# Two transformer blocks in float32: mixers rebuilt by head pairs, with two-pass float32r scores and normalised probabilities

## The chip, the cores and the metric

The kernel runs on one core of a Trainium2 chip. The metric is the device time of one execution in microseconds; three timed runs and one profiled execution of the kernel before are given. TensorE (PE) multiplies, VectorE (DVE), ScalarE (ACT) and GpSimd (POOL) do element work, SyncE (SP) issues most DMAs. Every engine works through its own instruction list in order, and the lists are tied together by semaphores that the kernel sets and waits for by hand.

## What is computed

Two different transformer blocks, one after the other, on 512 tokens of width 1024, all float32:

```python
# block 1: 12 heads of 64, three dilated branches (one table of log counts), RoPE, a pooling mixer of width 256
h = rms_norm(x, ln_pre_mix);  proj = h @ w_in                     # 1024 -> 256 + 3*768
mix = concat([multi_scale_pool(u), dilated_attention(rope(q), rope(k), v)]) @ w_out
x = x + rms_norm(mix);  x = x + rms_norm((silu(h2 @ w_gate) * (h2 @ w_up)) @ w_down)
# block 2: three kinds of attention; every q and k head is RMS-normed and scaled by a gain
a = softmax(q1 k1' + alibi) - lam * softmax(q2 k2' + alibi);  o_a = rms_norm(a @ v)     # 4 heads, 8 maps
o_b = softmax(q k' + F_q - F_k, causal) @ v                                             # 6 "fox" heads
o_c = softmax(q k' + rel_bias, chunks) @ v                                              # 6 "chk" heads
h = h + concat([o_a, o_b, o_c]) @ w_out_2;  h = h + conv_gated_mlp(rms_norm(h))
h = h + (p @ w_ple_proj) * sigmoid(rms_norm(h) @ w_ple_gate)
```

All attention is causal in steps, so of a map of 512 by 512 scores only 1, 2, 3 and 4 tiles of 128 keys are computed for the four blocks of 128 queries. There are 12 maps in block 1 and 8 + 6 + 6 = 20 in block 2.

## The kernel before

Everything stays in SBUF between the stages; only weights stream in, 1 MB at a time, into one of two slots (`w_raw`). Each large product is made in three float32r passes: a float32 number is split into a high part (`w_hi`, `h_hi`) and a rest (`w_lo`, `h_lo`), and hi*hi + hi*lo + lo*hi is summed in PSUM (`products`, lines 1337 to 1339; `row_tile`, lines 1482 to 1486). ACT makes the high part of weights (`split_hi`, L707), DVE the rest (`split_lo`, L932), in four quarters of 128x512 a chunk.

The order of the work is one list of steps for each mixer (`block1_plan`, `block2_plan`), and all engines walk through that same list, each doing its share of a step. The steps: `proj` (24 matmuls, 128 tokens by 256 columns; 9 chunks in block 1 and 15 in block 2, four tiles of tokens each), `rows` (DVE reads the bank: RoPE, norm or copy), `qkT` (PE turns q and k, DVE copies them out of bank 7, L1420 and L1062 to L1078), and for one unit, which is a map `m` and a block of queries `t`: `S` (scores in plain float32 from 64 feature rows, L1450; DVE adds the table and takes the maximum, L1171; ACT exponentiates in place, L764), `T` (PE turns the unnormalised probabilities, L1458; ACT copies them out, L771), `PV` (plain float32, the probabilities stationary and 64 columns of values moving, L1470; DVE scales by the reciprocal of the sum, L1184), and `mixT` (the finished heads turned, L1430). A unit's `T` comes two units behind its `S`, its `PV` three behind. The scores use two banks of PSUM by turns, the turned probabilities two more, the projections two, `PV` bank 6 and every other turn bank 7. The maps of a group of four to eight begin when three to five chunks are projected, with the projections of the next group between their units; the last group has the pool mixer or nothing between its units. `out` (0 to 3) are the first row products of `w_out`, put into the end of the list.

POOL has only small norms, the window means of the pool mixer (L639 to L653) and some DMAs.

Of the kernel before, what the change touches and what calls it, by code (L numbers as in the profile page):

```python
# [7 lines left out]
P = 128  # L8
S = 512
T = S // P  # L10
# [29 lines left out]
LEAD = 3  # L40
SECOND_MAP = (3, 1, 2, 0)

NORMED = ("diff_qk", "fox_qk", "chk_qk")
TURNED = ("q", "k") + NORMED

def parts(steps, heads):

    out = []
    for step in steps:  # L50
        if step[0] in heads or not out:
            out.append([])
        out[-1].append(step)
    return out

def interleave(attention, filler):

    units, fillers = parts(attention, ("S",)), parts(filler, ("proj", "poolproj", "poolmix"))  # L60
    out, done = [], 0
    for n, unit in enumerate(units):
        want = len(fillers) * (n + 1) // len(units)
        out += unit + sum(fillers[done:want], [])
        done = want
    return out + sum(fillers[done:], [])

def attention_steps(units, after):

    out = []
    for n in range(max([len(units) + 3] + [m + 4 for m in after])):
        if 0 <= n - 2 < len(units):
            out.append(("T", units[n - 2]))
        if n < len(units):
            out.append(("S", units[n]))
        if 0 <= n - 3 < len(units):
            out.append(("PV", units[n - 3]))
        out += after.get(n - 3, [])  # L80
    return out

def mixer_steps(groups, after, fillers, last_fillers):

    units = [u for maps in groups for m in maps[::2] for t in range(T) for u in ((m, t), (m + 1, SECOND_MAP[t]))]  # L90
    main = attention_steps(units, after)
    starts = [main.index(("S", (maps[0], 0))) for maps in groups]
    out = []
    for lo, hi, filler in zip(starts, starts[1:], fillers):
        out += interleave(main[lo:hi - LEAD], filler) + main[hi - LEAD:hi]
    lo, end = starts[-1], main.index(("S", units[-1])) + 2
    cuts = [lo + (end - lo) * n // len(last_fillers) for n in range(len(last_fillers) + 1)]
    for lo, hi, filler in zip(cuts, cuts[1:], last_fillers):
        out += interleave(main[lo:hi], filler)
# [3 lines left out]

def projection_steps(chunks, ends, extra=None):

# [1532 lines left out]
```

## Time and profile before

| | us |
|---|---|
| median of three runs | 1466.72 |
| lowest and highest | 1466.27, 1471.14 |
| span of the profiled execution | 1469.6 |
| TensorE busy in it | 1428.1 (97%) |
| VectorE / ScalarE / GpSimd busy | 714.2 / 525.4 / 125.8 |

The mixer of block 1 fills about 15 to 244 us of the span, that of block 2 about 656 to 996 us; between and behind them lie the output products and the two feed-forward parts. "Busy" PE time includes a modelled end of each matmul, so a row's mean is longer than the distance from one matmul to the next; the distance is read from the starts in the timeline.

### The profile page before, as it was taken

To read this page: it belongs to the slowest core of one execution; us is meant where nothing else is said; L and a number is where in the kernel's file an instruction comes from.
4 is the path that set the end of the run, shared out by engine and by line. 5 is a ranking of instruction groups with operands and counts; after the bars stand their busy time and mean duration, and the time that the engine had idled before them with its cause. 6 is when DMAs were issued, how large, how long until landed. Compare 5 with 4: busy or idle time off the path is not lost.

```text
span 1469.6 us, 21588 instructions
## 1 busy us (share of the span) xinstructions
PE 1428.1 (97%) x8040; PEld 1212.9 (83%) x8040; DVE 714.2 (49%) x1565; ACT 525.4 (36%) x1066; POOL 125.8 (9%) x205
## 2 busy tenths in 40 slices
PE   6999999899999999999999999999899999999999
PEld 6888877788888888879888899878888888888888
DVE  5655543632322333355546665445555555633454
ACT  4233343432222222343244344453533433423352
POOL 2000050300000000033302221000000000000000
PEclk9999999899999999999999999999999999999999
DMA  6111021232332322223210112103223223232312
GB/s 213 58 59 58 31 85 58 73 101 86 113 99 84 103 101 99 86 86 101 87 59 30 58 31 101 58 1 132 72 86 114 86 97 103 86 115 86 105 44 82
DMA packets 91225, 122.15 MB, mean 83 GB/s; under 512 B 3883, under 2 KB 81146, under 8 KB 90896
## 3 DMA queue, kind: packets, MB, share of 16 engines
q1 hardware_dynamic: 89616, 114.72, 23.5%
q0 software_dynamic: 1536, 6.45, 1.2%
q8 instruction: 47, 0.77, 0.2%
q14 instruction: 26, 0.21, 0.0%
HBM read 119.06 MB, written 2.10 MB: 82 GB/s over the span
## 4 chain that ended last, share of the span: by engine, by line
PE 52%; DVE 1%; POOL 1%; issue 1%; ACT 0%; DVEq 0%; ACTq 0%
PE ps L1337 10%; PE ps L1339 10%; PE ps L1338 10%; PE ps L1482 4%; PE ps L1484 4%; PE ps L1486 4%; PE ps L1450 4%; PE ps L1470 3%; PE ps L1458 2%; PE ps L1348 1%; POOL qk_rs L584 1%; DVE h_tok L967 0%; PE ps L1416 0%; PE ps L1420 0%; POOL qk_ss L583 0%
## 5 line engine op out<-in xcount | busy, mean ns | idle before, releaser
L932 DVE TENSOR_TENSOR w_lo<-w_raw,w_hi 128x512 fp32r<-128x512 f32 x416 | 269.8, 687 | 329.5 <-ACT w_hi L707 329.2
L707 ACT ACTIVATE w_hi<-w_raw 128x512 fp32r<-128x512 f32 x416 | 238.1, 621 | 307.9 <-PE ps L1486 192.8
L1337 PE MATMUL ps<-h_hi,w_hi 128*128 128x512 f32 (+1 forms) x752 | 288.2, 383 | 0.0
L1338 PE MATMUL ps<-h_lo,w_hi 128*128 128x512 f32 (+1 forms) x752 | 287.3, 382 | 0.0
L1339 PE MATMUL ps<-h_hi,w_lo 128*128 128x512 f32 (+1 forms) x752 | 287.2, 382 | 0.0
L1337 PE MATMUL ps<-w_hi,h_hi 128*128 128x256 f32 x896 | 262.5, 293 | 3.3 <-DVE work L1044 1.8
L1339 PE MATMUL ps<-w_hi,h_lo 128*128 128x256 f32 x896 | 255.0, 285 | 0.0
L1338 PE MATMUL ps<-w_lo,h_hi 128*128 128x256 f32 x896 | 254.9, 284 | 0.0
L1482 PE MATMUL ps<-w_hi,st_hi 128*128 128x512 f32 x464 | 181.5, 391 | 0.8 <-DVE st_lo L1197 0.7
L1484 PE MATMUL ps<-w_lo,st_hi 128*128 128x512 f32 x464 | 181.2, 391 | 0.0
L1486 PE MATMUL ps<-w_hi,st_lo 128*128 128x512 f32 x464 | 181.1, 390 | 0.0
L1337 PEld LDWEIGHTS ps<-w_hi,h_hi 128*128 128x128 f32 x896 | 173.3, 193 | 5.6 <-issue 3.4
L1338 PEld LDWEIGHTS ps<-w_lo,h_hi 128*128 128x128 f32 x896 | 173.4, 194 | 0.0
L1339 PEld LDWEIGHTS ps<-w_hi,h_lo 128*128 128x128 f32 x896 | 173.0, 193 | 0.0
L1337 PEld LDWEIGHTS ps<-h_hi,w_hi 128*128 128x128 f32 x752 | 143.2, 190 | 27.4 <-issue 0.9
L1339 PEld LDWEIGHTS ps<-h_hi,w_lo 128*128 128x128 f32 x752 | 143.0, 190 | 27.0
L1338 PEld LDWEIGHTS ps<-h_lo,w_hi 128*128 128x128 f32 x752 | 143.1, 190 | 26.7
L764 ACT ACTIVATE prob<-prob,neg_max 128x128 f32<-128x128 f32 (+3 forms) x128 | 71.9, 562 | 197.4 <-DVE neg_max L1171 197.2
L1482 PEld LDWEIGHTS ps<-w_hi,st_hi 128*128 128x128 f32 x464 | 87.5, 189 | 19.5 <-issue 1.1
L1486 PEld LDWEIGHTS ps<-w_hi,st_lo 128*128 128x128 f32 x464 | 87.5, 189 | 18.2
L1484 PEld LDWEIGHTS ps<-w_lo,st_hi 128*128 128x128 f32 x464 | 87.4, 188 | 18.1
L771 ACT ACTIVATE probT<-ps 128x128 f32<-128x128 f32 (+3 forms) x128 | 54.2, 423 | 21.3 <-PE ps L1458 20.6
(180 smaller groups left out, 1425.7 us busy)
## 6 DMA issues: line engine op xcount, KB each, us to landing
w_raw<-in_w_up_dram SPq DMA_DIRECT2D x33, 1024.0 KB, 5.1
w_raw<-in_w_in_dram SPq DMA_DIRECT2D x25, 1024.0 KB, 5.3
w_raw<-in_w_down_dram SPq DMA_DIRECT2D x22, 1024.0 KB, 4.8
w_raw<-in_w_gate_dram SPq DMA_DIRECT2D x11, 1024.0 KB, 5.2
w_raw<-in_w_out_dram SPq DMA_DIRECT2D x8, 1024.0 KB, 4.8
w_raw<-in_w_ple_gate_dram SPq DMA_DIRECT2D x4, 1024.0 KB, 5.6
x<-in_x_dram SPq DMA_DIRECT2D x4, 512.0 KB, 8.0
out_dram<-x SPq DMA_DIRECT2D x16, 128.0 KB, 1.7
```

Source lines behind the costliest of these rows:

```text
L707: act.activation(w_hi[:, slot, q], w_raw[:, slot, q], ACT.Copy).then_inc(hi_done, 1)
L764: act.activation(prob, prob, ACT.Exp, bias=neg_max[:, u % 8:u % 8 + 1], scale=-1.0, accum_out=den[:, u % 8:u % 8 + 1]).then_inc(exp_done, 1)
L771: act.activation((probT1, probT2)[mx.b][:, u % 2, 0:kn], ps[:, 4 + u % 2, 0:kn], ACT.Copy)\
L932: dve.tensor_tensor(w_lo[:, slot, q], w_raw[:, slot, q], w_hi[:, slot, q].bitcast(F32), ALU.subtract).then_inc(lo_done, 1)
L1337: pe.matmul(out_, s_hi, m_hi, start=(n == 0), stop=False)
L1338: pe.matmul(out_, s_hi, m_lo, start=False, stop=False)
L1339: mm = pe.matmul(out_, s_lo, m_hi, start=False, stop=(n == len(pairs) - 1))
L1450: pe.matmul(ps[:, 2 + u % 2, 0:P * (t + 1)], q[:, P * t:P * t + P], k[:, 0:P * (t + 1)], start=True, stop=True).then_inc(scores_done, 1)
L1470: mm = pe.matmul(ps[:, 6, 0:HD], probT[:, u % 2, P * j:P * j + P], v[:, j, :], start=(j == 0), stop=(j == t))
L1482: pe.matmul(bank, rows_hi[:, k, tok], hi[:, k, col], start=first and k == 0, stop=False, skip_group_check=True)
L1484: pe.matmul(bank, rows_hi[:, k, tok], lo[:, k, col], start=False, stop=False, skip_group_check=True)
L1486: mm = pe.matmul(bank, rows_lo[:, k, tok], hi[:, k, col], start=False, stop=last and k == RB - 1, skip_group_check=True)
```

## The change

Only the two mixers, the weights that feed them and the places of their buffers change.

- **Projection by head pairs.** A chunk is q, k and v of one pair of heads (384 columns; 512 for two differential heads, 262 for the differential values with the forget gates), loaded in two halves of four k-blocks. Each half is a `proj` of 12 matmuls for each tile of tokens; four banks (0 to 3) hold the four tiles.
- **Weight rests on POOL.** `weights_lo` (POOL) takes the place of DVE's `split_lo` in the mixers, in two pieces a load.
- **Scores in two float32r passes.** `turn` turns q or k of a pair for all tokens through bank 7; ACT copies the high part of each head into its rows of a ring tile, DVE writes the rest beside it, into the other 64 rows. For keys both parts are copied once more, so that q (hi over lo) times two stacked key tiles gives all products in two passes of 128 rows. Fox maps have a third pass for the decay.
- **Probabilities normalised first.** `N`: DVE takes the reciprocal, POOL multiplies the probabilities by it; in the differential maps `N2` (DVE) combines the two maps, so that one turn and one `PV` remain for two.
- **Split values stationary.** `T` turns into the single bank 6, ACT copies the high part (`pt_hi`), DVE the rest (`E`, `pt_lo`). `PV` is one step a map: 8 float32r matmuls of 512 down to 128 columns into bank 7; ACT and DVE add its two halves straight into `mixT`, so the `mixT` turns are left out except for the differential heads, which keep a float32 `PVd`.
- **Order.** Units start when their own pair is turned, at 1.1 (block 1) or 1.4 (block 2) units a projection slot.

```diff
+    for k, chunk in enumerate(chunks):
+        ...
+            for half in range(2):
+                for t in range(T):
+                    slots.add(n, ("proj", k, half, t))
+                    n += 1
...
+        ready[k] = n + (3 if normed else 2)
...
+        place = max(place + 1 / rate, ready[chunk_of(u[0])])
+        at.append(int(place))
...
+                    elif kind == "N":
+                        u, kn = mx.unit[s[1:]], P * (s[2] + 1)
+                        pool.wait_ge(rden_done, of["N"] + 1)
+                        p = prob[:, u % NPROB, 0:kn]
+                        pool.tensor_tensor(p, p, rden[:, u % 8:u % 8 + 1].to_broadcast([P, kn]), ALU.mult)\
+                            .then_inc(normed, 1)
...
+            def weights_lo(mx, n, piece):
+                c = mx.c0 + n
+                ...
+                pool.wait_ge(hi_done, 4 * c + 2 * (piece + 1))
+                q = half_piece(mx, n, piece)
+                pool.tensor_tensor(w_lo[:, c % 2, q], w_raw[:, c % 2, q], w_hi[:, c % 2, q].bitcast(F32), ALU.subtract)\
+                    .then_inc(lo_done, 2)
...
+                for i, tile in enumerate(tiles):
+                    rows, others = head_rows(i)
+                    dve.wait_ge(turn_hi_done, 2 * of["turn"] + i + 1)
+                    ins = dve.scalar_tensor_tensor(out=ring[rows if key else others, tile + key, :], in0=ps[rows, 7, :],
+                                                   scalar=turn_scale(mx, g, rows), in1=ring[rows, tile, :].bitcast(F32),
+                                                   op0=ALU.mult, op1=ALU.subtract)
+                ins.then_inc(bank7_read, 1)
...
+                    elif kind == "E":
+                        t = s[2]
+                        dve.wait_ge(pt_hi_done, mx.cnt.of["T", s[1], t]["six"] + 1)
+                        rows = slice(P * t, P * t + P)
+                        dve.tensor_tensor(pt_lo[:, 0:t + 1, rows], ps[:, 6, 0:P * (t + 1)].rearrange("p (j n) -> p j n", n=P),
+                                          pt_hi[:, 0:t + 1, rows].bitcast(F32), ALU.subtract).then_inc(pt_lo_done, 1)
...
+                        if fox:
+                            pe.matmul(bank, nid[:, m - 8:m - 7].to_broadcast([P, P]), ft[:, keys], start=True, stop=False)
+                        pe.matmul(bank, q, ring[:, tile + 1, keys], start=not fox, stop=False)
+                        pe.matmul(bank, q, ring[:, tile + 2, keys], start=False, stop=True).then_inc(scores_done, 1)
+                    elif kind in ("T", "T2"):
+                        ...
+                        if of["six"]:
+                            pe.wait_ge(pt_hi_done, of["six"])
+                        if of["E"]:
+                            pe.wait_ge(pt_lo_done, of["E"])
...
+                        pe.wait_ge(bank7_read, of["seven"])
+                        for j in range(T):
+                            v, later = vs[:, (pair + 1) % 3, j, hh, :], slice(P * j, S)
+                            pe.matmul(ps[:, 7, later], v, pt_hi[:, j, later], start=j == 0, stop=False,
+                                      skip_group_check=True)
+                            mm = pe.matmul(ps[:, 7, later], v, pt_lo[:, j, later], start=False, stop=j == T - 1,
+                                           skip_group_check=True)
```

Three places of the order. First PE in the mixer of block 1, where the maps of the first pair end: before, the end of the first maps' units among projections (`v`, `probT`, `qk` are values, turned probabilities and turned q and k).

```order
L1420 MATMUL ps<-ident,work_70 128x128 x2
L1450 MATMUL ps<-qk_66 128x128
L1470 MATMUL ps<-v_67,probT_69 128x64 x3
L1458 MATMUL ps<-ident,prob_68 128x128 x4
L1450 MATMUL ps<-qk_66 128x128
L1470 MATMUL ps<-v_67,probT_69 128x64 x3
L1458 MATMUL ps<-ident,prob_68 128x128
```

After the change the turn of the second pair's keys (L1604) stands directly ahead of the first map's PV (L1668, L1670; `vs` is the split values), and both use bank 7.

```order
L1604 MATMUL ps<-ident,work_75 128x128 x4
L1668 MATMUL ps<-pt_hi,vs 128x512
L1670 MATMUL ps<-pt_lo,vs 128x512
L1668 MATMUL ps<-pt_hi,vs 128x384
L1670 MATMUL ps<-pt_lo,vs 128x384
L1668 MATMUL ps<-pt_hi,vs 128x256
L1670 MATMUL ps<-pt_lo,vs 128x256
L1668 MATMUL ps<-pt_hi,vs 128x128
L1670 MATMUL ps<-pt_lo,vs 128x128
L1658 MATMUL ps<-ident,prob 128x128 x4
```

Eight PV matmuls took the place of the many small ones, and between two uses of bank 7 there is nothing on PE.

Second, PE at the end of the mixer of block 1, behind the row product `out 1`, after the change.

```order
L1658 MATMUL ps<-ident,prob 128x128 x3
L1644 MATMUL ps<-ring_83 128x512
L1645 MATMUL ps<-ring_83 128x512
L1658 MATMUL ps<-ident,prob 128x128 x2
L1644 MATMUL ps<-ring_83 128x384
L1645 MATMUL ps<-ring_83 128x384
L1658 MATMUL ps<-ident,prob 128x128
L1644 MATMUL ps<-ring_83 128x256
L1645 MATMUL ps<-ring_83 128x256
L1668 MATMUL ps<-pt_hi,vs 128x512
```

Between one `T` (L1658, bank 6) and the next stand only the two score passes of a later unit (L1644, L1645).

Third, POOL as the first attention units of block 1 begin, after the change (before, POOL had nothing here between its DMAs and the window means).

```order
L795 TENSOR_TENSOR w_lo<-w_raw,w_hi 128x768 x6
L745 TENSOR_TENSOR prob<-prob,rden 128x512
L795 TENSOR_TENSOR w_lo<-w_raw,w_hi 128x768
L745 TENSOR_TENSOR prob<-prob,rden 128x384
L795 TENSOR_TENSOR w_lo<-w_raw,w_hi 128x768
L745 TENSOR_TENSOR prob<-prob,rden 128x256
L745 TENSOR_TENSOR prob<-prob,rden 128x128
```

The rests of the weights and the probabilities' normalising now share one queue.

## Rows read from the trace of the kernel before

**Rows 1.** The page: its first lines, busy us (share) and instructions.

```profile
span 1469.6 us, 21588 instructions
PE 1428.1 (97%) x8040; PEld 1212.9 (83%) x8040; DVE 714.2 (49%) x1565; ACT 525.4 (36%) x1066; POOL 125.8 (9%) x205
```

**Rows 2.** Windows of the middle of both mixers: length, busy us (instructions) by engine, clock, DMA.

```profile
60.00:221.00 161.00, 160.11 (x1069) 129.98 (x1069) 86.80 (x297) 59.28 (x162) 18.68 (x24) 1.00 0.16 53
733.00:962.00 229.00, 228.14 (x1655) 195.62 (x1653) 131.57 (x471) 100.08 (x270) 37.13 (x58) 1.00 0.16 54
```

**Rows 3.** Timeline of PE, projection: start, us, then the start of the next.

```profile
22.94 0.28 PE L1338 MATMUL ps<-w_lo,h_hi 128*128 128x256 f32 x1
23.06 0.28 PE L1339 MATMUL ps<-w_hi,h_lo 128*128 128x256 f32 x1
```

**Rows 4.** Timeline of PE, 512 columns in the row products.

```profile
540.56 0.39 PE L1486 MATMUL ps<-w_hi,st_lo 128*128 128x512 f32 x1
540.79 0.39 PE L1482 MATMUL ps<-w_hi,st_hi 128*128 128x512 f32 x1
```

**Rows 5.** Timeline of PE, units of the last maps with no filler.

```profile
953.97 0.28 PE L1458 MATMUL ps<-ident,prob 128*128 128x128 f32 x1
954.18 1.12 PE L1450 MATMUL ps<-qa 64*128 64x512 f32 x2
955.23 1.10 PE L1470 MATMUL ps<-va,probT 128*128 128x64 f32 x8
956.17 0.28 PE L1458 MATMUL ps<-ident,prob 128*128 128x128 f32 x1
956.38 0.70 PE L1450 MATMUL ps<-qa 64*128 64x256 f32 x2
957.01 0.43 PE L1470 MATMUL ps<-va,probT 128*128 128x64 f32 x2
957.28 0.60 PE L1458 MATMUL ps<-ident,prob 128*128 128x128 f32 x4
957.82 0.70 PE L1450 MATMUL ps<-qa 64*128 64x256 f32 x2
```

**Rows 6.** Groups by line and form: count, busy us, mean ns, idle before.

```profile
L1243 DVE SCALAR_TENSOR_TENSOR act_gate<-ps,conv_cols,act_gate 128x510 f32<-128x510 f32 x22 | 16.5, 749 | 2.6
L1171 DVE CUSTOM_DVE_ANT_0 prob<-ps,table 128x384 f32<-128x384 f32 x14 | 7.7, 553 | 3.6 <-PE ps L1450 3.6
L771 ACT ACTIVATE probT<-ps 128x512 f32<-128x512 f32 x32 | 18.7, 585 | 8.4 <-PE ps L1458 8.4
L764 ACT ACTIVATE prob<-prob,neg_max 128x384 f32<-128x384 f32 x32 | 19.7, 615 | 54.0 <-DVE neg_max L1171 53.9
L764 ACT ACTIVATION_READ_ACCUMULATOR prob<-prob,neg_max 128x1 f32 x128 | 23.9, 187 | 0.0
L640 POOL TENSOR_TENSOR pool_a<-pool_u 128x511 f32<-128x511 f32 x2 | 2.1, 1037 | 0.2
L653 POOL TENSOR_TENSOR pool_d<-pool_d,pool_u 128x512 f32<-128x512 f32 x2 | 2.5, 1272 | 0.2
```

**Rows 7.** End of block 1's mixer: windows as in rows 2, then PE's timeline.

```profile
221.00:243.00 22.00, 19.47 (x91) 15.74 (x90) 8.49 (x26) 6.66 (x16) 0.00 (x0) 0.84 0.00 1
...
226.00:228.00 2.00, 2.00 (x9) 1.68 (x9) 0.30 (x2) 0.98 (x3) 0.00 (x0) 0.50 0.00 0
...
224.54 0.99 PE L1470 MATMUL ps<-v,probT 128*128 128x64 f32 x4 [1.70 <-DVE otok L1184]
```

**Rows 8.** One instruction's line: ns min/median/max; POOL's addition and DVE's scaling in the norms.

```profile
L609 POOL TENSOR_TENSOR x<-x,y_scaled x8: 725/1321/1445, 273.0 to 658.6; 128x256 f32<-128x256 f32 x8
L967 DVE SCALAR_TENSOR_TENSOR h_tok<-x,x_rs,gain_pre x20: 1279/1286/1752, 6.8 to 1410.0; 128x1024 f32<-128x1024 f32 x20
```

**Rows 9.** Timeline of all engines: a score product and DVE's reading of it.

```profile
977.77 1.12 PE L1450 MATMUL ps<-qa 64*128 64x512 f32 x2
...
978.93 0.69 DVE L1171 CUSTOM_DVE_ANT_0 prob<-ps,table 128x512 f32<-128x512 f32 x1 [0.96 <-PE ps L1450]
```

More of the change, by code:

```diff
@@ L69, in attention_steps @@
[L69 to L99, printed above, removed]
-    t1, pv1 = main.index(("T", units[-1])), main.index(("PV", units[-1]))
-    out += main[end:t1] + [("out", 0)] + main[t1:pv1] + [("out", 1)] + main[pv1:pv1 + 1] + [("out", 2)]
-    return out + main[pv1 + 1:] + [("out", 3)]
@@ new lines, with columns @@
+KH = KB // 2
+PAIRS = 6
+NPROB = 4
+FALLING = (3, 2, 1, 0)
+POOL_PARTS = 4
+CAUSAL_TABLE = 4
+def columns(chunk):
+    kind = chunk[0]
+    if kind == "qkv":
+        return [(256 + 768 * j + P * chunk[1], P) for j in range(3)]
+    if kind == "pool":
+        return [(0, 256)]
+    if kind == "d":
+        return [(256 * j + P * chunk[1], P) for j in range(4)]
+    if kind == "dv":
+        return [(DIFF_V, 256), (FOX_GATE, 6)]
+    base = FOX if kind == "fox" else CHK
+    return [(base + 384 * j + P * chunk[1], P) for j in range(3)]
@@ L191, in __init__ @@
             kind = s[0]
-            if kind in ("proj", "poolproj", "poolmix"):
+            if kind in ("proj", "out") or kind == "poolproj" and s[3] == POOL_PARTS - 1:
                 self.n["product"] += 1
+            if kind == "rows" or kind == "poolproj" and s[3] == POOL_PARTS - 1:
                 self.n["bank"] += 1
-            elif kind in ("qkT", "mixT", "decay"):
-                self.n["turn"] += 1
-            elif kind == "S":
-                self.n["unit"] += 1
-            elif kind == "out":
-                self.n["product"] += 1
+            if kind in ("turn", "PV", "PVd", "mixT", "decay", "poolmix"):
+                self.n["seven"] += 1
+            if kind in ("turn", "S", "sum", "E", "T2", "N", "N2", "PV", "PVd", "combine"):
+                self.n[kind] += 1
+            if kind in ("T", "T2"):
+                self.n["six"] += 1
+            if kind == "turn" and s[2] % 2:
+                self.n["keys"] += 1
 def two_blocks_kernel(nc, A, out):
@@ new lines, in two_blocks_kernel, with raw_count, more_dmas, chunk_of_map @@
+        m.buffer_free = {key: consumer.get(u - NPROB) for key, u in m.unit.items()}
+        mixers.append(m)
+    dmas = [1] * C_END
+    for m in mixers:
+        for n, (k, kb0, kbs) in enumerate(m.loads):
+            dmas[m.c0 + n] = len(columns(m.chunks[k]))
+    def raw_count(c):
+        return 16 * sum(dmas[c % 2:c + 1:2])
+    def more_dmas(b, slot):
+        first = (C_UP1, C_UP2)[b]
+        c = first + (slot - first) % 2
+        return raw_count(c) - (8 * c + 16 - 8 * (c % 2))
+    def chunk_of_map(b, m):
+        if b == 0:
+            return chunks1.index(("qkv", m // 2))
+        return chunks2.index(("d", m // 4) if m < 8 else ("fox", (m - 8) // 2) if m < 14 else ("chk", (m - 14) // 2))
```

1153 lines of the change are left out of this document (651 added, 502 removed).

## Prediction

> **What bounds the kernel now.** I read the page first: PE is busy for 97% of a span of 1469.6 us, DVE for 49%, ACT for 36%, POOL for 9% [rows 1]. Then the windows of the two mixers, since only they change: between 60 and 221 us PE is busy 160.1 of 161 us, between 733 and 962 us 228.1 of 229; DVE is at 54 and 57% there [rows 2]. So in the mixers nothing waits for anything but PE, and a change is worth what it takes off PE's list, less what it makes PE wait. Then the timeline, for the distance from one matmul to the next, which is what a matmul costs.
>
> **Prices on PE.** A 256-column float32r matmul comes every 0.12 us [rows 3], a 512-column one every 0.23 (0.227 over several) [rows 4]; the slope is 0.42 ns a column, so 384 columns cost 0.173 and 262 cost 0.122. From starts in the unit stretch [rows 5]: S 1.05 us for 512 keys and 0.63 for 256, so 0.84 for 384 and 0.42 for 128, in sum 2.94 for a map. PV: 0.94 for eight small matmuls and 0.27 for two, so 0.49 and 0.72 between, 2.42 a map. T: 0.21 for one turn, 0.54 for four, 1.5 a map. A map costs 6.9 us of PE, and 32 of them 220.
>
> **What leaves PE.**
> - Projection: before 24 chunks of 96 matmuls, 2304 x 0.120 = 276.5. After 1152 of 384 columns, 192 of 512, 96 of 262: 199.3 + 43.6 + 11.7 = 254.6. Gain 21.9, 18 of it in block 2, which projected overlapping columns; wider matmuls alone give little, because the time is nearly all columns.
> - Scores: a map is two passes of 512, 384, 256 and 128 columns. No row shows a float32r matmul of 128 columns. Lower bound the slope (0.067), upper half the float32 pair of S at 128 keys (0.21); I take 0.12, the 256-column row, its nearest. With 0.1 for the change of mode (an estimate: the fixed part of the two matmuls of S is 0.21 in rows 5) the map is 1.68. 32 maps: 94.1 to 53.8, plus a third pass in six fox maps, 3.8. Gain 36.5.
> - PV: 24 maps x (8 matmuls, 1.28, + 0.1) = 33.1, and the differential heads, now one float32 PV for two maps, 4 x 2.42 = 9.7; before 77.4. Gain 34.6.
> - Turns of probabilities: 4 maps fewer, 6.0. Turns of q and k: 52 pairs of 0.32 and 12 fours of 0.54, 23.1, become 32 fours, 17.3: 5.8. mixT: 12 of 14 leave, 6.5.
> - Against it: 24 more beginnings of a group of projections at the same 0.1, 2.4, and 1 for the decay's small products.
>
> Sum: 21.9 + 36.5 + 34.6 + 6.0 + 5.8 + 6.5 - 3.4 = **108 us** less work on PE, about 36 in block 1 and 72 in block 2. The 118 float32r matmuls of 128 columns make it 98 to 114.
>
> **Do the other engines carry it?** For a head pair of block 1 PE needs 26.8 us (16.6 projection, 1.1 turns, 9.1 for two maps). DVE: RoPE and the value rests 6.8, ring rests 4 x 0.75 and key copies 2 x 0.55, scores 2 x 2.3, reciprocals 1.2, `E` 2 x 1.95, PV 2 x 0.69, together 22; ACT 18.6 (exponentials 2 x 3.0, copies of probabilities 2 x 1.7, of PV 1.2, of the ring 3.6, of values 1.1, weights 3.3), by [rows 6]. POOL: a 512-wide operation takes 1.04 to 1.27, so a 768-wide weight rest about 1.6, four of them and two maps of normalisation at 3.1 give 12.6. Though DVE is freed of the weight rests, its share rises to about 80%. In block 2 a fox pair comes to 27 us of DVE and 15 to 21 of POOL in 30 to 32 of PE. So no engine takes PE's place as the bound by its sum. The gain can be lost only in **waits**.
>
> **What PE now waits for.** Before, two banks held scores, two the turned probabilities, and PV had its own. After, all turned probabilities go through bank 6, and turns of q and k, PV, PVd, mixT, poolmix and decay through bank 7, each alone in it. The order shows where two uses follow closely.
> - *Bank 7 behind a turn.* ACT's two copies of 512 (0.585 and, overlapped, 0.49), DVE's second rest 0.75, and handovers of 0.1 [rows 6, 9] give 2.2 if ACT is free; but in ACT's list the exponential of the newest unit (0.6 + 0.19) stands ahead. I take 2.6; bounds 1.9 and 3.4. Behind PV (ACT 0.585, DVE 0.69) 1.7. Against the PE work standing between, block 1 has nine short places: four with nothing between (a turn of keys directly ahead of a PV, 2.6 each), one of 2.05, four of 0.5 to 0.7: 14.7. Block 2 has fifteen: six of 2.6, three of 1.13 in the first differential chunk, the rest 0.2 to 1.9: 23.6.
> - *Bank 6.* The next T waits for ACT's copy and DVE's `E`, and `E` stands behind the newest unit's scores in DVE's list: S 0.45, handover 0.1, table and maximum 0.63, `E` 0.49, handover: 1.75 behind a T. Where no projection lies between, PE has only S, 0.35 to 0.55. 14 places in block 1 (14.0), 19 in block 2 (21.3), half of this in the two tails, where the eight last units have only three row products as filler.
>
> Taken together, since a wait for one bank also lets the other empty, 28 and 45: **73 us**. With round trips 0.7 as long it is 42, with 1.3 as long 110. Queued behind PE's wait is everything: projections, and with them the weights that ACT and POOL prepare.
>
> The drain of the last map (T, `E`, PV, both readers, `out 3`) is longer than before by some 3 us for both mixers; nothing to nine is possible. Start of the kernel: the first half chunk has less to split, but its second half waits for POOL; 0, between -1 and +2.
>
> **The clock.** Before, one wait of 1.70 us that ended at 224.5 was followed by a window at clock 0.50, that is 1.2 GHz in place of 2.4, and the 22 us from 221 to 243 had a mean of 0.84 [rows 7]: 0.16 x 22 = 3.5 us of lost work, some 7 us at the lower level. The change puts about 14 waits of two us or more into streams of projections. But where PE waits anyway, a slow clock costs less. I take five such falls, **17 us**; bounds 0 and 48.
>
> **The sum.** 1469.6 - 108 + 73 + 3 + 17 = 1454.6 of span. The median of the runs lay 2.9 under the profiled span; so **1452 us**.
>
> **POOL beside DVE.** In the norms POOL's 128x256 addition took 725 ns at best and 1445 at worst, DVE's scaling with two SBUF inputs 1279 and 1752, where they ran beside each other [rows 8]. In the mixers before, POOL was almost idle; now it works half the time beside DVE's RoPE sums, key copies and `N2` (two SBUF inputs, or a copy within SBUF).
> The Trainium skill, SBUF — State Buffer, section "Who interferes with whom", says that these two share a pair of ports as an exclusive lock and that the later one is blocked for the whole instruction; the maxima in rows 8 agree with it in kind. That rule speaks against moving weight rests to POOL, and is what the second rival below would rest on.
>
> **Rivals.**
> 1. *Not faster, by the clock.* Each of 14 long waits starts a stretch at 1.2 GHz: 48 in place of 17, span 1485.6, **1483 us**. It decides once more than nine falls occur (108 - 73 - 3 = 32 us is what they have to eat, 3.5 each). For it: rows 7. Against: many falls would overlap. 0.22.
> 2. *Slower, by POOL and DVE holding each other up.* Some 96 DVE operations of the kinds named above, blocked for 0.3 to 0.5 us each on the average, 29 to 48 us; that DVE can carry, but it lies in the round trips of both banks and makes them 1.3 as long: 110 in place of 73, span 1491.6, **1489 us**. It decides when round trips grow by a quarter. 0.15.
> 3. *The queues hide it.* ACT and DVE catch up while PE projects, turns cost 1.9, waits 42, no fall: 1469.6 - 108 + 42 + 3, **1404 us**. For it: ACT is at 70% of PE's work in a pair and DVE at 80, so both have time to catch up. 0.22.
> 4. *The forecast*, 1435 to 1465: 0.41.
>
> **Range and chances.** 1400 to 1503 takes in the third case down to its own value, both slow ones and 10 us for the narrow matmuls, and leaves out the sum of all good ends (1395 and less) and of all bad ones. What a measurement of this kernel can tell from no change is 0.3%, 4.4 us. Faster: the third case, and nearly all of the forecast's, 0.59. Same: 0.08. Slower: 0.33, from rivals 1 and 2, less a little that falls short.
>
> **What would show it.** In the profile after: matmuls of 384 columns every 0.17 us and S with 512 keys in 0.55; PE's idle time in the two mixers about 60 to 80 us against 1.8 in the windows of rows 2, put down to DVE (the readers of banks 6 and 7) at the lines of T, turn and PV; PE's waits of 2 to 3 us directly behind a turn; windows at clock 0.5 inside the mixers, a handful; the feed-forward parts as before. Wrong I would be if PE waits for weights (POOL's `w_lo`) or for normalised probabilities, if the 128-column passes take 0.2 us, or if the idle time is under 40 us.

## The result, and the profile after

The changed kernel takes **1502.4 us** (median of 4 runs, 1501.6 to 1508.9) against 1466.7 before: a ratio of 1.0243, 95% interval 1.0217 to 1.0269. It is 2.4% slower; the forecast was 1452, faster. The profiled execution has a span of 1499.4 us.

The first lines of the page answer to [rows 1]:

```profile
span 1499.4 us, 18918 instructions
PE 1350.4 (90%) x6732; PEld 1164.5 (78%) x6732; DVE 718.9 (48%) x1473; ACT 605.4 (40%) x1171; POOL 308.2 (21%) x361
```

PE lost 78 us of busy time, and the span still grew by 30. The stage boundaries on PE's timeline tell where: the first mixer, with the start, ended at 245.5 us and now ends at 261.8 (+16.3); the second took 344.6 and takes 358.7 (+14.1); the feed-forward parts did not move by more than half a us. The windows of the two mixers (columns as in [rows 2]: PE, PE's weight loads, DVE, ACT, POOL, then the mean granted clock):

```profile
0.00:261.81 261.81, 204.54 (x1068) 183.46 (x1069) 141.04 (x385) 121.11 (x264) 112.01 (x121) 0.92 0.23 71
667.46:1026.19 358.73, 284.04 (x1574) 254.69 (x1573) 193.10 (x542) 187.25 (x412) 168.63 (x190) 0.92 0.19 55
```

PE idles 57.3 and 74.7 us, 132.0 in all; over the same two stages of the kernel before it idled 16.8 and 7.7. And the clock fell from 0.99 to 0.92. Both can be put into one account. In windows of 2 us I took, in each, PE's busy time times (1 - granted clock) as what the lower level (1.2 GHz in place of 2.4) added to the busy time; busy time less that is PE's work at full clock. For the two mixers together:

| | PE busy | idle | added by the clock | work at full clock |
|---|---|---|---|---|
| before | 565.6 | 24.5 | 5.9 | 559.7 |
| after | 488.6 | 132.0 | 38.5 | 450.1 |
| difference | -77.0 | +107.5 | +32.6 | -109.6 |

So the work left as forecast (108), and waits and clock brought back 140. Who is waited for, from the view of PE's waits (us in total, times, longest), the main ones inside the mixers:

```profile
PE ps L1658 <- DVE pt_lo L1368: 47.4, 33, 3.5
...
PE ps L1668 <- DVE ring L1252: 16.7, 6, 3.1
PE ps L1604 <- DVE ring L1252: 9.5, 12, 2.5
PE ps L1692 <- DVE out_lo L1329: 5.3, 1, 5.3
PE ps L1680 <- DVE ring L1252: 5.2, 2, 2.7
PE ps L1668 <- DVE vs L1243: 4.9, 4, 1.5
PE ps L1668 <- DVE pt_lo L1368: 4.1, 3, 2.6
...
PE ps L1518 <- POOL w_lo L795: 2.9, 3, 1.5
```

L1658 is T, the transposes of probabilities into bank 6, and `pt_lo` is `E`, the last reader of that bank. L1604 is turn, L1668 PV, L1680 PVd, and `ring` L1252 the last reader of bank 7 behind a turn. L1692 is the first row product of block 2's output. Weights are hardly waited for.

Now the longest wait at T in block 1, the second T of the first map, on the timeline of all engines (PE's projections and other rows left out). It shows what stands ahead of `E`:

```profile
51.28 0.60 PE L1658 MATMUL ps<-ident,prob 128*128 128x128 f32 x4
...
52.47 0.51 ACT L951 ACTIVATE prob<-prob,neg_max 128x256 f32<-128x256 f32 x1 [2.56 <-DVE neg_max L1299]
...
52.98 0.83 ACT L865 ACTIVATE w_hi<-w_raw 128x768 fp32r<-128x768 f32 x1
...
53.72 0.26 ACT L907 ACTIVATE vs<-ps 128x128 fp32r<-128x128 f32 x1
...
53.87 0.59 ACT L959 ACTIVATE pt_hi<-ps 128x512 fp32r<-128x512 f32 x1
...
53.96 1.81 POOL L795 TENSOR_TENSOR w_lo<-w_raw,w_hi 128x768 fp32r<-128x768 f32 x1 [0.54 <-ACT w_hi L865]
54.01 0.42 DVE L1222 TENSOR_TENSOR work<-ps,rope_cos 128x256 f32<-128x256 f32 x1 [1.50 <-ACT vs L907]
...
54.86 1.18 DVE L1227 TENSOR_TENSOR work<-work,rope_part 128x256 f32<-128x256 f32 x1
...
56.37 0.68 DVE L1368 TENSOR_TENSOR pt_lo<-ps,pt_hi 128x512 fp32r<-128x512 f32 x1
...
57.20 0.52 PE L1658 MATMUL ps<-ident,prob 128*128 128x128 f32 x3 [3.01 <-DVE pt_lo L1368]
```

The transposes end at 51.88. Their first reader, ACT's copy, starts only at 53.87, because ACT's list has three things ahead of it: the newest unit's exponential (L951), for which ACT itself waited 2.56 us for DVE, the weight split and the projection's value copy (L907). DVE could subtract at 54.46, but its list first has the RoPE rows of the projection of the same slot, which waited for that value copy; and one addition of them (L1227) takes 1.18 us in place of 0.43 beside POOL's 1.81 us. `E` starts at 56.37, and the next T starts 5.3 us after this one ended.

This wait is not the usual one. Over the 33 waits at T for `pt_lo`, the median time from the end of one T to the start of the next is 1.82 in the first mixer and 1.89 in the second, near the 1.75 of the forecast. Only 6 of the 33 have a projection between the two T, as here, and they make 8.4 of the 47.4 us; the other 27, with no projection between, make 39.0.

A values product behind a turn, same view:

```profile
66.09 0.63 PE L1604 MATMUL ps<-ident,work 128*128 128x128 f32 x4 [0.29 <-DVE ring L1252]
...
67.69 1.19 ACT L938 ACTIVATE ring<-ps 64x512 fp32r<-64x512 f32 x2
68.29 1.39 DVE L1252 SCALAR_TENSOR_TENSOR ring<-ps,ring 64x512 fp32r<-64x512 f32 x2 [1.61 <-ACT ring L938]
...
69.83 0.76 PE L1668 MATMUL ps<-pt_hi,vs 128*128 128x512 f32 x1 [3.11 <-DVE ring L1252]
```

PE has nothing between the two uses of bank 7 and waits 3.11 us; at 106.88 and 182.86 it is 3.1 again. Here too ACT has an exponential (66.45) and a weight split (66.95) ahead of its copies.

### The profile page after: what moved, and what is told of

It reads as the page before. It is cut to its first block, busy times and chain, and to the rows that moved or that the text cites. A ratio compares the mean times of both kernels' runs of the same rounds, so it can differ in the third digit from the quotient of the medians.

```text
span 1499.4 us, 18918 instructions
## 1 busy us (share of the span) xinstructions
PE 1350.4 (90%) x6732; PEld 1164.5 (78%) x6732; DVE 718.9 (48%) x1473; ACT 605.4 (40%) x1171; POOL 308.2 (21%) x361
## 4 chain that ended last, share of the span: by engine, by line
PE 43%; DVE 5%; issue 2%; POOL 2%; ACT 2%; DVEq 0%; ACTq 0%; POOLq 0%
PE ps L1518 9%; PE ps L1520 9%; PE ps L1519 9%; PE ps L1692 4%; PE ps L1694 4%; PE ps L1696 4%; DVE ring L1252 2%; PE ps L1658 1%; ACT ring L938 1%; POOL w_lo L795 1%; POOL qk_rs L702 1%; PE ps L1604 1%; PE ps L1530 1%; DVE pt_lo L1368 1%; PE ps L1645 1%
## 5 line engine op out<-in xcount | busy, mean ns | idle before, releaser
L1137 DVE TENSOR_TENSOR w_lo<-w_raw,w_hi 128x512 fp32r<-128x512 f32 x312 | 199.0, 687 | 267.5 <-ACT w_hi L853 267.4
L853 ACT ACTIVATE w_hi<-w_raw 128x512 fp32r<-128x512 f32 x312 | 176.0, 622 | 284.3 <-PE ps L1696 195.0
L1518 PE MATMUL ps<-w_hi,h_hi 128*128 128x384 f32 (+3 forms) x608 | 208.7, 343 | 4.2 <-POOL w_lo L795 2.9
L1519 PE MATMUL ps<-w_lo,h_hi 128*128 128x384 f32 (+3 forms) x608 | 204.2, 336 | 0.0
L1520 PE MATMUL ps<-w_hi,h_lo 128*128 128x384 f32 (+3 forms) x608 | 204.2, 336 | 0.0
L1692 PE MATMUL ps<-w_hi,st_hi 128*128 128x512 f32 x464 | 181.6, 391 | 0.0
L795 POOL TENSOR_TENSOR w_lo<-w_raw,w_hi 128x768 fp32r<-128x768 f32 (+2 forms) x62 | 118.4, 1912 | 63.3 <-ACT w_hi L865 62.2
L1519 PEld LDWEIGHTS ps<-w_lo,h_hi 128*128 128x128 f32 x608 | 119.1, 196 | 3.5 <-issue 0.5
L1520 PEld LDWEIGHTS ps<-w_hi,h_lo 128*128 128x128 f32 x608 | 118.6, 195 | 2.8
L951 ACT ACTIVATE prob<-prob,neg_max 128x512 f32<-128x512 f32 (+3 forms) x128 | 72.2, 564 | 117.3 <-DVE neg_max L1299 116.5
L745 POOL TENSOR_TENSOR prob<-prob,rden 128x512 f32<-128x512 f32 (+1 forms) x96 | 69.9, 728 | 188.6 <-DVE rden L1353 188.1
L1692 PEld LDWEIGHTS ps<-w_hi,st_hi 128*128 128x128 f32 x464 | 87.5, 189 | 18.4 <-DVE h_lo L1178 0.3
```

Source lines behind the costliest of these rows:

```text
L745: pool.tensor_tensor(p, p, rden[:, u % 8:u % 8 + 1].to_broadcast([P, kn]), ALU.mult)\
L795: pool.tensor_tensor(w_lo[:, c % 2, q], w_raw[:, c % 2, q], w_hi[:, c % 2, q].bitcast(F32), ALU.subtract)\
L853: act.activation(w_hi[:, slot, q], w_raw[:, slot, q], ACT.Copy).then_inc(hi_done, 1)
L951: act.activation(p, p, ACT.Exp, bias=neg_max[:, u % 8:u % 8 + 1], scale=-1.0, accum_out=den[:, u % 8:u % 8 + 1]).then_inc(exp_done, 1)
L1137: dve.tensor_tensor(w_lo[:, slot, q], w_raw[:, slot, q], w_hi[:, slot, q].bitcast(F32), ALU.subtract).then_inc(lo_done, 1)
L1518: pe.matmul(out_, s_hi, m_hi, start=first and n == 0, stop=False, skip_group_check=True)
```

## The experiments

Two theories. **Order:** a bank is freed late because of what stands ahead of its readers in the written order, and because two uses of one bank stand next to each other; moving steps, with no work changed, wins the time back. **Lock:** the readers are late because POOL and DVE hold each other up, wherever the steps stand (the second rival). A third question was whether the clock falls because of the idle stretches (the first rival). All kernels below start from the changed kernel, compute the whole result, and were timed against the kernel before on the same chip. The kernel before had medians of 1466.7 to 1470.8 us in the different groups of runs (e1 to e4; e5 to e8; e9 to e11; e12), so times of different groups are compared by their ratios to it, and a difference of 2 to 4 us between raw medians of two groups says nothing.

### Moving steps within their slot

Each slot of the plan is a list of steps; e1 to e3 sort it. For e3:

```
-    out = sum(slots.at, [])
+    late_kinds = ('sum', 'rows', 'decay_abs', 'decay_ln', 'decay_log', 'turn')
+    out = [s for slot in slots.at for s in [x for x in slot if x[0] not in late_kinds]
+                                         + [x for x in slot if x[0] in late_kinds]]
```

e1 has all these kinds but `turn`, e2 `turn` alone. e4 leaves the slots as they are and moves `E` in `unit_steps`:

```
     if plain(n - 3):
         out.append(("T",) + at(n - 3))
+    if plain(n - 3):
+        out.append(("E",) + at(n - 3))
     ...
     if at(n):
         out.append(("S",) + at(n))
-    if plain(n - 3):
-        out.append(("E",) + at(n - 3))
```

> Edit: within each slot of the plan the projection's evacuation (rows, sum and the decay steps) stands behind the slot's unit steps instead of ahead of them, on every engine; nothing is added or left out. Order theory (VectorE reaches the low part of the transposed probabilities, the reader that frees bank 6, only behind the rows of the projection that the same slot computes): the 47.4 us that TensorE waits for that reader fall to about half, mixer idle 132 us to about 105, time about 1475 to 1490. Lock theory (VectorE is late because GpSimd's operations hold the port, wherever its steps stand): the wait stays above 40 us and the time at 1495 to 1505. A third outcome: the bank of the projection comes free later and TensorE waits there instead, idle unchanged.

Measured: 1500.8 us, ratio to before 1.0220 (1.0198 to 1.0242). The changed kernel had 1.0243 (1.0217 to 1.0269), so no difference is shown. The expectation of the order theory (1475 to 1490, the wait at T halved, idle 105 us) did not come; the time is in the range of the lock theory, and the idle time, 126.4, nearest to the third outcome.

> Edit: within each slot only the turns (transposes of queries, keys through bank 7) stand behind the unit steps, so that no turn stands directly ahead of a values product that needs the same bank. If the round trip of bank 7 is what is paid at the products that wait 3.1 us behind a turn (some eight of them, 25 us), these waits go and the time falls by 15 to 25 us, to about 1480. If the wait only moves to the next user of bank 7 (the next turn behind the product), the idle time stays at 125 to 135 us and the time within 5 us of 1502.

Measured: 1478.3 us, 1.0057 (1.0038 to 1.0076), 24 us less than the changed kernel (27 by the ratios).

> Edit: both of the moves above at once (rows and turns behind the unit steps of their slot). Order theory: the gains add, mixer idle about 85 to 95 us, the clock higher in the tails of the mixers, time about 1455 to 1475. Lock theory: 1490 to 1505.

Measured: **1461.4 us**, 0.9957 (0.9943 to 0.9970), 41 us less than the changed kernel and 0.4% faster than the kernel before. The idle time, 105.9, is above the 85 to 95 that were expected.

> Edit: within the unit steps the evacuation E of the transposed probabilities stands directly behind the transposes T, ahead of the next unit's scores S (on TensorE nothing moves, since E is not TensorE's; on VectorE and ScalarE the readers of bank 6 come ahead of the readers of the newest scores). Order theory: the wait for the low part falls from 47.4 to 30 to 40 us, the exponential starts later by as much and costs nothing, time 1490 to 1500. Lock theory: no change, 1500 to 1505.

Measured: 1508.9 us, 1.0275 (1.0255 to 1.0295): slower by 6.5 us, or 5 by the ratios, where 1490 to 1500 was expected; the intervals of the two ratios still overlap.

The order theory holds for e2 and e3; e1 and e4 missed. In e2 the waits at PV behind a turn fell from 16.7 to 4.8 us and the one of 5.3 us at the first row product to 0.4, while the wait at T stayed at 47.0. PE's waits of e1, where only the rows moved:

```profile
PE ps L1659 <- DVE pt_lo L1369: 37.7, 27, 3.5
...
PE ps L1605 <- DVE vs L1244: 14.2, 6, 3.7
```

The wait at T fell by 9.7 us, where some 24 were expected, and the turn at the head of the next slot (L1605) now waits for the late rows, 14.2 us against 1.3. With the turns late too, in e3:

```profile
PE ps L1659 <- DVE pt_lo L1369: 36.9, 28, 1.9
...
PE ps L1605 <- DVE vs L1244: 7.8, 5, 2.2
...
PE ps L1669 <- DVE ring L1253: 3.7, 4, 2.3
```

No wait at T is over 1.9 us, and the long ones at PV behind a turn are gone (16.7 to 3.7). So moving the rows alone gives nothing (5.6 us less idle time, 6.6 more by the clock), moving the turns alone 24 us, and both together 41: the rows' part only shows when the turns no longer wait for them. The windows of e3's two mixers:

```profile
0.00:241.99 241.99, 196.60 (x1068) 177.12 (x1069) 133.69 (x385) 121.38 (x264) 113.13 (x121) 0.95 0.25 77
647.64:987.74 340.10, 279.60 (x1574) 248.46 (x1573) 195.25 (x542) 185.52 (x412) 168.30 (x190) 0.94 0.21 59
```

Idle 105.9 in place of 132.0, and the clock adds 25.0 in place of 38.5: of 40 us, a third is clock.

In e4 the idle time is the same as after (132.6). The wait at T is lower by 7.7 us (39.7), but the waits at the turns for `ring` and `vs` grew from 10.8 to 15.7 and those at PV for `vs` from 4.9 to 7.2. What made it slower is what the clock adds, 38.5 to 45.9. Why it adds more at equal idle time, no run here settles.

### The lock

> Edit: the rests of the mixers' weights (w_lo) are formed on VectorE again, as in the kernel before, and not on GpSimd; the values are the same. Lock theory (GpSimd's 1.8 to 2.4 us operations hold VectorE up ahead of the readers that free banks 6 and 7): TensorE's waits on VectorE fall by 20 us or more and the time to 1480 or less, although VectorE has more to do. Order theory (VectorE is late by what stands ahead of these readers in its own order): VectorE gets about 25 us of work more in the mixers, ahead of the same readers; the time stays at 1500 or rises to 1520.

```
+            def weights_lo(mx, n, piece):
...
+                dve.tensor_tensor(w_lo[:, c % 2, q], w_raw[:, c % 2, q], w_hi[:, c % 2, q].bitcast(F32), ALU.subtract)
```

Measured: 1517.6 us, 1.0318 (1.0301 to 1.0336), 15 us more than the changed kernel (11 by the ratios). Yet the lock is there: the RoPE addition in the changed kernel and in e5 (ns min/median/max).

```profile
L1227 DVE TENSOR_TENSOR work<-work,rope_part x24: 424/426/2119, 31.6 to 211.4; 128x256 f32<-128x256 f32 x24
```

```profile
L1229 DVE TENSOR_TENSOR work<-work,rope_part x24: 424/425/635, 30.0 to 213.4; 128x256 f32<-128x256 f32 x24
```

With POOL freed of the weight rests, no such addition is over 0.64 us, where one took 2.12 before. By the Trainium skill, SBUF — State Buffer, section "Who interferes with whom", a VectorE instruction with two inputs in SBUF contends with a GpSimd instruction that reads SBUF; here the traces agree. But the wait at T stayed at 46.8 us, the idle time grew by 8.5 us and what the clock adds by 7.8: the 44 us more that DVE has to do (about 25 were expected) cost more than the lock did.

How large the lock is can be read from the same additions in the changed kernel and in e3 (us in total, mean ns):

```profile
L1227 DVE TENSOR_TENSOR work<-work,rope_part 128x256 f32<-128x256 f32 x24 | 20.5, 856 | 0.8
```

```profile
L1228 DVE TENSOR_TENSOR work<-work,rope_part 128x256 f32<-128x256 f32 x24 | 13.3, 556 | 0.8
```

Ten of the 24 are lengthened in the changed kernel, by 10 us together; in e5 the 24 take 10.4 us. All of DVE's operations in the two mixers, each against the usual time of its kind, come to some 16 us in 18 operations, where the second rival had 96 operations and 29 to 48 us. So its mechanism is real and a third to a half as large as it supposed. It isn't wholly separated from the order: in four of the six waits at T with a projection between (57.2, 92.7, 170.2 and 207.1, 7.9 us together) a lengthened addition stands ahead of `E`, and e3 lost 7 us of the lengthening by its moves. e2 had all of it (20.5 us) and still gained 24.

> Edit: rows and turns behind the unit steps (1461.4 us) and the rests of the mixers' weights on VectorE. If the lock with GpSimd is what is left of the waits (36.9 us for the low part of the transposed probabilities), the time falls to 1445 or less; if what is left is the round trip of one bank by itself, VectorE's added work only adds, 1460 to 1475.

The same edit on top of e3. Measured: 1474.8 us, 1.0030 (1.0018 to 1.0041), 13.4 us more than e3 (11 by the ratios); the wait at T is 39.8 in place of 36.9. Again DVE's added work costs more than it relieves.

### The clock

> Edit: ahead of the four values products of the first mixer that wait about 3.1 us each behind a turn, 36 products of 128 columns without use are put (into columns of bank 3 that nothing else uses), 36 x 0.06 = 2.2 us of work in place of 2.2 us of idle time. If the falls of the clock to half come from these idle stretches, the windows 60 to 110 and 180 to 190 us stay at 1.00 and the first mixer is 4 to 8 us shorter (time about 1495). If the clock falls wherever TensorE's load is low over more than these stretches, or for another reason, the windows stay at 0.83 to 0.86 and the time at 1500 to 1505.

```
                         pair, hh = (m - 8 * mx.b) // 2, m % 2
+                        if mx.b == 0 and m in (0, 2, 6, 8):
+                            for _ in range(36):
+                                pe.matmul(ps[:, 3, 384:512], h_hi[:, 0, 0:P], h_hi[:, 1, 0:P], start=True, stop=True, ...)
```

Measured: 1503.0 us, 1.0238 (1.0197 to 1.0278), no difference in the total. The fillers were dearer than I wrote: their pitch is 0.11 and not 0.06, so a group of 36 took 4.1 us and overran its wait. The windows of PE's clock still answer the question; first the changed kernel, then e6:

```profile
90.00:100.00 10.00, 7.99 (x36) 6.80 (x34) 7.44 (x25) 2.93 (x9) 1.42 (x3) 0.83 0.27 79
100.00:110.00 10.00, 5.68 (x27) 4.79 (x27) 4.52 (x12) 6.70 (x14) 5.50 (x4) 0.86 0.20 55
180.00:190.00 10.00, 7.14 (x27) 6.98 (x28) 3.86 (x9) 4.83 (x10) 3.04 (x3) 0.66 0.31 107
```

```profile
50.00:60.00 10.00, 7.02 (x38) 6.50 (x37) 7.42 (x23) 3.70 (x11) 5.37 (x5) 0.88 0.23 78
...
100.00:110.00 10.00, 8.86 (x67) 8.08 (x66) 4.98 (x12) 6.95 (x13) 5.26 (x4) 1.00 0.22 64
180.00:190.00 10.00, 9.36 (x65) 8.80 (x64) 4.38 (x10) 4.04 (x9) 2.11 (x2) 1.00 0.32 105
210.00:220.00 10.00, 8.30 (x40) 8.33 (x40) 4.30 (x10) 4.04 (x9) 1.26 (x2) 0.56 0.01 2
```

Where PE worked through the waits at 103 and 178 us, the clock stayed at 1.00, as it did from 70 to 100; the expected gain in time did not come. DVE's `E` of the same unit, in the changed kernel and in e6, gives what it was worth:

```profile
66.33 0.29 DVE L1368 TENSOR_TENSOR pt_lo<-ps,pt_hi 128x128 fp32r<-128x128 f32 x1
...
215.50 0.28 DVE L1368 TENSOR_TENSOR pt_lo<-ps,pt_hi 128x128 fp32r<-128x128 f32 x1
```

```profile
68.43 0.28 DVE L1368 TENSOR_TENSOR pt_lo<-ps,pt_hi 128x128 fp32r<-128x128 f32 x1
...
211.94 0.28 DVE L1368 TENSOR_TENSOR pt_lo<-ps,pt_hi 128x128 fp32r<-128x128 f32 x1
```

e6 was 2.1 us behind at 68 us, by a fall at 50 to 60 us ahead of the first filler that the changed kernel did not have there, and 3.6 us ahead at 212: it gained 5.7 us, although its fillers took longer than the waits. Then the last group of fillers met the lower level, took 7.9 us in place of 4.1, and lost the gain again. So in this pair of traces the falls went where the waits were filled, and the place of a single fall is partly chance: the two programs are the same up to the first filler. It is one trace of each. What else there is points the same way: the changed kernel's mixers have 18 separate falls (stretches below 1.00 in windows of 2 us) against 2 before, and each begins during or within 3 us behind a wait of 1.1 to 3.5 us. Not every such wait is followed by one: the 3.01 us ahead of 57.20 are not.

### E first once more

> Edit: rows and turns behind the unit steps of their slot (1461.4 us) and E directly behind T besides, which alone made the kernel 6.5 us slower. If that loss came because the exponential and then the transposes of the next units start later (the chain S, exponential, N, T has no room), it stays: 1466 to 1470. If it came only with the rows ahead of E, it turns: 1455 to 1460.

Measured: 1465.2 us, 0.9972 (0.9954 to 0.9989), 3.9 us more than e3, 2 by the ratios; the intervals overlap, so neither a loss nor the gain to 1455 to 1460 is shown. Its wait at T is 31.0 against 36.9 in e3, its turns wait 3.1 us longer for the rows, and the idle time is the same 105.9. To bring one reader forward only moved the wait.

### Fewer handovers

The transposes of a map's last two tiles (256 and 128 keys) become one step in bank 6. The core of the edit, in `unit_steps` (for `T` and for `E`) and on PE:

```
-    if plain(n - 3):
+    if plain(n - 3) and at(n - 3)[1] != 1:
...
+                        if kind == "T" and s[2] == 0:
+                            u = mx.unit[s[1], 1]
+                            for j in range(2):
+                                tr = pe.transpose(ps[:, 6, P * j + P:P * j + 2 * P], prob[:, u % NPROB, P * j:P * j + P], ident[:, :])
```

> Edit to the changed kernel: the transposes T of a map's last two tiles (256 and 128 keys) are one step through bank 6 (columns 0 to 383), with two copies on ScalarE and two subtractions on VectorE behind it, so that 24 of 80 handovers of bank 6 are gone and no work is. Order theory (TensorE pays for each handover of bank 6 that has less than about 3 us of other work between): the waits at T for the low part fall from 47.4 (33 waits) to 30 to 38, time 1488 to 1495. If bank 6 only hands its wait to the next user of bank 7 (the values product needs the same low parts, one step later), the waits at the values product behind it grow by as much: 1498 to 1505.

Measured: 1487.1 us, 1.0119 (1.0087 to 1.0151), 15.3 us less than the changed kernel (18 by the ratios). (There are 96 handovers behind a T, not 80; 24 of them went.) The wait at T for the low part fell by 25 us, from 47.4 to 22.3, more than expected, but the idle time by 10.1 only: 6.3 us of waits for normalised probabilities came up, since the merged step needs the newest of them, and two of the waits at PV grew (for `vs` 4.9 to 9.3, without a releaser in the profile 2.3 to 6.2). So more than half of the wait moved to the next steps, as the second expectation had it in kind.

> Edit: rows and turns behind the unit steps (1461.4 us) and the last two tiles' transposes in one step. Here 28 waits of at most 1.9 us for the low part are left (36.9 us in all). If they are the round trip of the bank itself (transposes end, ScalarE's copy, VectorE's subtraction), a third to a half of them goes: time 1442 to 1452. If they are the lateness of VectorE, 1458 to 1463.

Measured: **1442.1 us** (1441.6 to 1444.1), ratio to before 0.9810 (0.9794 to 0.9827). The best version: 1.9% faster than the kernel before, 4.0% faster than the changed one. PE's waits at T and two others, and the windows of its mixers:

```profile
PE ps L1668 <- DVE pt_lo L1378: 11.7, 8, 1.9
PE ps L1683 <- issue: 10.9, 8, 3.0
PE ps L1614 <- DVE vs L1249: 10.2, 5, 3.6
...
PE ps L1668 <- POOL prob L748: 4.4, 3, 1.5
```

```profile
0.00:232.41 232.41, 194.26 (x1069) 177.13 (x1069) 134.75 (x385) 120.19 (x266) 112.91 (x121) 0.95 0.26 79
638.06:968.51 330.45, 275.96 (x1577) 248.32 (x1575) 195.16 (x542) 184.36 (x412) 168.62 (x191) 0.95 0.20 58
```

Of the 36.9 us at T in e3, 25 went with a quarter of the handovers. The idle time fell by half of that, 105.9 to 92.6: waits for `prob` (4.4) came up, those at PV (L1683) with no releaser in the profile grew from 4.2 to 10.9, those at the turns for `vs` from 7.8 to 10.2. With that the time, 1442.1, is at the lower end of what was expected if the round trip of the bank is what is left.

### Units earlier or later

> Edit: the kernel with both moves and the merged transposes, and units placed earlier in the plan (rate 1.4 and 1.8 units a slot in place of 1.1 and 1.4), which leaves 10 in place of 11 score products behind the last projection in each mixer. If the uncovered tail of a mixer is what costs, a gain of 2 to 5 us over the same kernel without it; if units closer together lose their cover from projections, a loss of 5 to 15 us.

Measured: 1458.1 us, 0.9918 (0.9887 to 0.9950), 16 us more than e10.

> Edit: the kernel with both moves and merged transposes (1442.1 us), and units placed later in the plan (rate 1.0 and 1.2 units a slot in place of 1.1 and 1.4), which leaves 12 and 14 score products behind the last projection in place of 11 and 11. Placed earlier (1.4 and 1.8) they cost 16 us, with more waits between units. Cover theory: each unit now has more projection work beside it and the waits inside go down, while the tails get longer: between 1437 and 1450. If the uncovered tail decides, 1450 to 1460.

Measured: 1444.0 us (1439.7 to 1444.3), 0.9823 (0.9806 to 0.9839), the same as e10. Units packed closer lose the projections between them: in e11 the idle time is 102.4 in place of 92.6, with nearly all of the difference ahead of the last projection, and the clock adds 26.0 in place of 21.6. Spread wider, in e12, PE idles 5.3 us less ahead of the last projection of the mixers and 3.3 more behind it, 90.7 in all, with no difference in the time. The expectation that was on record for e12 held (1437 to 1450).

### All in one account

The same account as above, both mixers, in us:

| kernel | time | idle | added by the clock | work at full clock |
|---|---|---|---|---|
| before | 1466.7 | 24.5 | 5.9 | 559.7 |
| changed | 1502.4 | 132.0 | 38.5 | 450.1 |
| e1, rows late | 1500.8 | 126.4 | 45.1 | 448.0 |
| e2, turns late | 1478.3 | 116.0 | 30.6 | 452.2 |
| e3, both | 1461.4 | 105.9 | 25.0 | 451.2 |
| e4, E first | 1508.9 | 132.6 | 45.9 | 450.1 |
| e5, weights on VectorE | 1517.6 | 140.5 | 46.3 | 449.8 |
| e9, merge | 1487.1 | 121.9 | 37.4 | 447.8 |
| e10, both and merge | 1442.1 | 92.6 | 21.6 | 448.6 |
| e12, e10 with units later | 1444.0 | 90.7 | 19.8 | 448.5 |

The last column tests the account: with the same products the work comes out at 448 to 452 in nine traces, whatever the waits. All that moves the time is in the two columns before it, and they mostly move together: fewer waits, fewer falls. (The account is of the profiled execution, the time the median of all.)

## Why the prediction was wrong

**The work, right.** 108 us forecast, 109.6 measured. 384 columns come every 0.17 us, for instance in the changed kernel's timeline

```profile
53.16 0.33 PE L1519 MATMUL ps<-w_lo,h_hi 128*128 128x384 f32 x1
...
53.33 0.33 PE L1520 MATMUL ps<-w_hi,h_lo 128*128 128x384 f32 x1
```

S with 512 keys takes 0.54 (0.55 forecast). The 128-column passes, for which I had bounds 0.067 and 0.21 and took 0.12, cost 0.06 to 0.11, as the next row's start after each shows in e6:

```profile
73.73 0.23 PE L1672 MATMUL ps<-pt_hi,vs 128*128 128x128 f32 x1
73.79 0.27 PE L1674 MATMUL ps<-pt_lo,vs 128*128 128x128 f32 x1
73.90 0.29 PE L1658 MATMUL ps<-ident,prob 128*128 128x128 f32 x1
```

**The waits, too small: the step that failed first.** It is the term of 73 us, with 3 for the drain: 107.5 measured. It falls into three parts.

*Bank 7 behind turns* came out near: 33.9 us at the lines of PV, turn, PVd and mixT for `ring` (16.7, 9.5, 5.2, 2.5), against 38, though a single one took 3.1 where I had 2.6.

*Bank 6* did not: 51.5 us (47.4 at T, 4.1 at PV) against 35. The number of waits at T was the forecast's 33, and where no projection lies between two T the trip was its trip, 1.82 against 1.75. What was wrong there is the price of one wait. By the forecast's own figures, 1.75 less 0.35 to 0.55 of scores, it is 1.2 to 1.4, and 33 of them are 40 to 46, not 35; the prediction doesn't say how it came to less. Measured were 1.44 each at those 27, 39.0 in all (two of them have long trips too: 4.2 us at 878.2, where the copies of a turn stand ahead in both lists, and 3.0 at 965.3, behind rows). The other 6, 8.4 us, are a mechanism that the forecast put at nothing. It assumed that a projection between two T covers the trip. But the rows of a projection (those behind the second half of a chunk) stand ahead of `E` in DVE's list, the value copy ahead of the copy of `pt_hi` in ACT's, and the trip becomes up to 5.3 us: in this order the projection also delays it. e1, where the rows moved, took 9.7 us off the wait at T, and e3 left 0.7 us at T behind a projection.

*Some 22 us* more than before the forecast did not have at all. Behind them stand one wait of 5.3 us at the first row product behind a turn (0.4 in e2 and e3, whose turns are late), and waits for value rests (7.1), for rows of q and k (3.8), for head outputs (3.0), for POOL's weight rests (2.9) and for merged probabilities (2.1), and PE's own restarts.

"Do the other engines carry it?" was answered by sums, and the sums held: DVE's busy time in the mixers is 74% of PE's work at full clock (334 of 450 us; about 80 forecast), 54% of their length. They say nothing of when a reader's turn comes.

**The clock, too small: the other step.** 17 forecast, bounds 0 and 48, 32.6 measured. The number of falls was over the first rival's 14, not near my five: 18 separate ones against 2 before. By the granted clock of the 2 us windows the mixers spend 96 us at the lower level against 14 before. "Where PE waits anyway, a slow clock costs less" was right: those 96 us would add 48 if PE were busy all the time, and added 38.5, 2.1 a fall and not 3.5. The error is the number of falls. The forecast counted 14 waits of two us or more where its own list has 11; measured are 20 in the mixers, against 2 before.

Together 1454.6 + 31.5 + 15.6, less the 1.6 by which the work fell further: 1500.1, the profiled span to within 1 us. So of the 44.8 us between forecast and measured span, two thirds are waits and one third is clock. That the time still lies inside 1400 to 1503 is no merit of the forecast: the range was drawn to hold both slow rivals.

**The rivals.** The first (by the clock) had the right mechanism and half of its size: it put 31 us on top of the forecast, and 15.6 came. The second (POOL and DVE) gave nearly the measured sum of waits, 110, and with 1489 the nearest time, but by luck: what it builds on lengthened DVE's operations by some 16 us and not 29 to 48, the trip of bank 6 without a projection kept its 1.82, and in e5 and e8, where 116 of POOL's 281 us in the mixers were taken away, the waits stayed. The third (the queues hide it) was out: a turn ahead of a PV costs 3.1, not 1.9. What no run separates is how much of the 7.9 us of waits behind lengthened additions would be left without the lock and with DVE's work unchanged.

**What would show it.** PE's idle time in the mixers was named as the mark, 60 to 80; 132.0, which is 107.5 more than before, told that the waits and not the work were off. Waits for POOL's `w_lo` came to 2.9 us, and the feed-forward parts stayed.

## What to carry to other kernels

When a bank is shared, list for each engine that reads it everything that stands ahead of the reader in that engine's written order, the steps of other streams too, and what those wait for; a sum of busy times per engine doesn't price this. Look first at two uses of one bank that stand next to each other: parting them was the largest single gain here (24 us in e2). Before giving up a change that turns an engine from 97% busy into one that waits, try to move steps within their slots and to merge the shortest handovers: here, with no product changed, it was worth 60 us, from 2.4% slower to 1.9% faster. But judge such a move by the total idle time and not by the one wait that it aims at: in e1, e4, e7, e9 and e10 part or all of the wait came back at the next step. Idle time on PE was paid for a second time through the clock, in the changed kernel with another 0.3 us for each us (32.6 to 107.5) and in the others with 0.2 to 0.4, so a change that adds waits has to win more than their sum.

## What the runs showed of the hardware that I had not expected

- A 128-column float32r product stands 0.06 us from its partner with the same number of columns, and 0.11 from what comes next; 36 in a row have a pitch of 0.11 in e6 (0.21 at the lower clock). In a row they are hardly cheaper than products of 256 columns (0.12 in [rows 3]).
- An addition of 128x256 on DVE with both inputs in SBUF, 0.42 us, took up to 2.12 beside POOL's 768-wide operation of 1.85 us that had begun 0.01 us before it.
- Two kernels that are the same up to 66 us had a fall of the clock at 50 to 60 us in one (e6, 0.88) and none in the other (the changed kernel, 1.00).
